# A two-layer diffusion backbone on one core: which modulation pairs, output products and attention steps run ahead of the gathers, and in what order

## Chip, core and metric

The kernel runs on 1 core of a Trainium2 chip. The metric is device time in microseconds (us) of one execution; the number given for a kernel is the median of several executions. All arithmetic is float32.

## The reference, cut to what matters

Two layers over 256 latent tokens and 256 context tokens of width 1024. Layer 0 has a gated-conv and spatial-gating mixer, layer 1 a conv module beside differential attention (4 heads); each is followed by PEER, a lookup of 128 expert rows per token. Every sub-layer is modulated by six vectors made from `c` (or `c_ctx`).

```python
for l in range(2):
    ada_x = (silu(c) @ w_ada[l] + b_ada[l]).reshape(1, 1, 6, 1024)
    ada_c = (silu(c_ctx) @ w_ada[l] + b_ada[l]).reshape(1, 1, 6, 1024)
    hx = modulate(rms_norm(x, norm1_g[l]), ada_x[:, :, 0], ada_x[:, :, 1])
    ...
    x = x + ada_x[:, :, 2] * yx
    h2 = modulate(rms_norm(x, norm2_g[l]), ada_x[:, :, 3], ada_x[:, :, 4])
    x = x + ada_x[:, :, 5] * peer(h2, ...)

def diff_attend(q, k, v, lam):           # layer 1, per head
    p = softmax(einsum(q, k) * 64 ** -0.5)
    return einsum(p[:, :, 0] - lam * p[:, :, 1], v)

def peer(h, wq, subkeys, u_tab, v_tab):  # per token
    q = h @ wq                           # 8 heads, 2 halves of 128
    s = q . subkeys; top 16 of each half; top 16 of their 256 sums -> idx, g
    return sum over the 128 idx of  g * gelu(h . u_tab[idx]) * v_tab[idx]
```

## The kernel before

**Stages and slots.** There are three stages of PEER work: stage 0 (latent tokens, layer 0), stage 1 (context tokens, layer 0), stage 2 (latent tokens, layer 1). Each has two tiles of 128 tokens, and each tile 128 slots. In a slot GpSimd issues one indirect DMA that gathers, for 128 tokens, one row of u and one of v (1 MB) into one of 8 ring slots of `uv`. VectorE multiplies u with the token row and sums (L1557, a dot), ScalarE makes a weight of it and a diagonal matrix (L1189 to L1193), and TensorE adds diag times v into two PSUM banks (`add_values`, L948), two slots later in its own program. 768 slots in all.

**Order.** `schedule()` writes one list, the program; every engine walks the same list and does its part of each step. A step may be "taken" (its PSUM bank emptied) later than it is issued. Dense steps are either placed between slots (`placed`, spread over a range of slots) or written out by hand in `before[stage]`, ahead of a stage's first slot. `before[0]` is the opening: nothing can be gathered until the first tile has passed through the mixer, the norm, `query`, `score` and the six parts of `find`, the search that writes `idx`. `before[2]` is the gap: the first tile of stage 2 needs the end of stage 1, the attention of layer 1 and the same chain. `deal(a, b)` spreads the steps b evenly among the steps a.

**Modulation vectors.** There are 12 pairs of columns per layer (a pair is two blocks of 1 MB, 8 KB per partition). A pair comes either on TensorE (`ada`, L680, then `ada_turn`, L695 and L696) or on VectorE (`ada_row`, L1250: a transposed block, two chunks, each multiplied with the two rows `c_rows` and summed). Layer 0 uses pairs 0 to 3 for shift and scale of the mixer, 4 and 5 for its gate, 6 to 9 for shift and scale of PEER, 10 and 11 for PEER's gate. `ADA_ROWS` says which pairs VectorE makes. `c_rows` is loaded by a DMA (L969) and passed through Silu on ScalarE (L1167) in step `mods`, just ahead of the first `norm`.

**Weights.** All blocks stream through the SyncE queue in program order (L983). `weight_places` gives each a place: 3 slots of `wring`, or, in the opening and in the gap, ring slots of `uv`. A block whose place is still held waits in the queue, and all behind it. In the gap the ring slots 2 to 5 may be used (`GAP_SLOTS`); slots 6 and 7 (`LATE_SLOTS`) hold the attention's `vc_rows[1]`, `orow[1]`, `pT`, `prob`, and their first gathers wait for step `o_turn` of the second tile, by this line of the GpSimd program:

```python
if T and s == LATE_SLOTS[0]:
    pool.wait_ge(*taken["orow", 1])
```

**Attention steps.** For i = 0 to 7 (tile, head): `scores` (PE, L836), `smax` (DVE, L1435), `soft` (ACT, L1095), `mix` (DVE, L1442 to L1444), `p_turn` (PE, L845), `value` (PE, L855). After a tile's four heads come `o_norm` (DVE), `o_turn` (PE, L871), and `out_half` (PE, L893; two halves b, four products each).

Of the kernel before, what the change touches and what calls it, by code (L numbers as in the profile page):

```python
# [43 lines left out]
ADA_ROWS = ((0, 10, 12), (1, 0, 6))  # L44
# [10 lines left out]

GAP_SLOTS = (2, 3, 4, 5)
LATE_SLOTS = (6, 7)
# [114 lines left out]
def kept_heads(stage):  # L172
# [6 lines left out]
         "rms_sum": 1.5, "rms_root": 1, "rms_scale": 1.5, "norm": 3, "out_half": 4, "turn_back": 2, "lam": 1, "conv": 2,  # L179
# [28 lines left out]
def schedule():  # L208
# [29 lines left out]

    early = [(0, 1, [mix[7], p_turn[7], value[7]]), (1, 2, [("o_norm", 2, 1)]), (2, 3, [("o_turn", 2, 1)]), (2, 10, find(2, 1, one)),
# [70 lines left out]
def weight_blocks(program):  # L310
# [3 lines left out]
    for i, (kind, item, *_) in enumerate(program):  # L314
# [7 lines left out]
        elif name == "out_half":  # L322
# [18 lines left out]
def weight_places(program, blocks):  # L341


    own, opening, gap = list(range(WRING)), list(range(WRING + RING)), list(range(WRING)) + [WRING + i for i in GAP_SLOTS]

    found = [program.index(("step", step)) for step in (("query", 0, 1, 0, (0,)), ("find", 2, 0, (0,), FIND_PARTS - 1))]
# [3 lines left out]
    for k, (_, _, _, first, last) in enumerate(blocks):  # L350
# [1302 lines left out]
```

## Time and profile before

| | |
|---|---|
| time, median of 3 runs | 2381.09 us (2379.73 to 2384.25) |
| the profiled execution: its own time, its span | 2382.0 us, 2380.2 us |
| PE, DVE, ACT, POOL busy | 2080.4 (87%), 1629.1 (68%), 961.4 (40%), 1021.0 (43%) us |
| DMA moved, mean | 940.46 MB, 395 GB/s |
| indirect gathers | 768, 805.36 MB |
| chain that ended last | PE 36%, DMA 29%, DVE 16%, issue 7%, POOL 6%, ACT 4% |

Times within the trace are counted from the start of its span. The span and 1.8 us around it make the execution's time. Busy time is the sum of an engine's instructions; the DMA share is the mean busy share of the core's 16 DMA engines.

### The profile page before, as it was taken

What the parts mean: (1) busy time and instruction counts of PE and PEld (TensorE: products, weight loads), DVE (VectorE), ACT (ScalarE), POOL (GpSimd) and SP (SyncE); (2) the same over time, 40 slices, a digit from 0 to 9 for tenths busy, and PEclk for the clock granted to TensorE, in tenths of its full rate; (3) what the DMA queues carried; (4) which work ended last, traced back from release to release, by engine and by line L of the source; (5) the groups of instructions that cost most, each with busy time, mean ns of one, the idle gap of its engine ahead of it and who ended that gap; (6) DMA issues with size and microseconds to landing.
All of it is one profiled execution on the core that took longest, in us unless ns stands there. A gap on an engine that the chain in (4) does not pass through costs nothing.

```text
span 2380.2 us, 23945 instructions
## 1 busy us (share of the span) xinstructions
PE 2080.4 (87%) x6792; PEld 1119.3 (47%) x6792; DVE 1629.1 (68%) x3980; ACT 961.4 (40%) x2788; POOL 1021.0 (43%) x868
## 2 busy tenths in 40 slices
PE   8988998899998988988899998898799987777777
PEld 6775554455564434544454454335456532222222
DVE  2876768967766568788856668754665887766444
ACT  2113434543334444444454334534443444443333
POOL 0002444444334544444445445520233555566774
PEclk9998999999999999999999999999899999999999
DMA  9968999999999999999999999994599999999997
GB/s 402 420 252 320 394 415 421 414 422 422 421 421 421 412 421 405 421 419 420 389 406 422 421 421 421 421 381 192 224 403 379 415 421 421 422 421 421 421 421 319
DMA packets 132738, 940.46 MB, mean 395 GB/s; under 512 B 14736, under 2 KB 17936, under 8 KB 18960
## 3 DMA queue, kind: packets, MB, share of 16 engines
q0 software_dynamic: 110592, 805.36, 82.0%
q1 hardware_dynamic: 22032, 133.73, 13.7%
q8 instruction: 54, 0.88, 0.1%
q14 instruction: 60, 0.49, 0.1%
HBM read 937.98 MB, written 1.05 MB: 395 GB/s over the span
## 4 chain that ended last, share of the span: by engine, by line
PE 36%; DMA 29%; DVE 16%; issue 7%; POOL 6%; ACT 4%; SPq 0%; POOLq 0%; DVEq 0%; ACTq 0%
DMA uv<-uv_dram,stage_idx 28%; PE psum L948 18%; PE psum L762 9%; POOL uv L1019 6%; DVE uv L1557 6%; PE psum L744 4%; DVE h L1250 2%; PE psum L893 1%; DMA h<-c_rows_dram 1%; ACT diag L1193 1%; ACT wv L1191 1%; PE psum L680 1%; ACT gel L1189 1%; DVE work L1521 0%; PE psum L922 0%
## 5 line engine op out<-in xcount | busy, mean ns | idle before, releaser
L948 PE MATMUL psum<-uv,diag 128*128 128x512 f32 x3072 | 1449.8, 612 | 240.0 <-ACT diag L1193 221.8
L1019 POOL DMA_INDIRECT uv<-uv_dram,stage_idx x768 | 987.2, 1285 | 1051.7 <-PE psum L948 823.7
L1557 DVE CUSTOM_DVE_ANT_0 uv<-uv,h 128x1024 f32<-128x1024 f32 x768 | 935.2, 1226 | 538.1 <-DMA uv<-uv_dram,stage_idx 527.4
L948 PEld LDWEIGHTS psum<-uv,diag 128*128 128x128 f32 x3072 | 562.7, 193 | 1023.7 <-issue 518.1
L1189 ACT ACTIVATE gel<-dots 128x1 f32<-128x1 f32 x768 | 156.3, 203 | 1052.4 <-DVE dots L1557 1050.2
L1193 ACT ACTIVATE diag<-const,wv 128x128 f32<-128x128 f32 x768 | 309.8, 403 | 24.8
L762 PE MATMUL psum<-hT,wring 128*128 128x256 f32 (+1 forms) x1280 | 266.2, 362 | 1.5 <-ACT hT L1060 1.5
L762 PEld LDWEIGHTS psum<-hT,wring 128*128 128x128 f32 x1280 | 227.9, 191 | 59.7 <-issue 33.0
L1191 ACT ACTIVATE wv<-gel,gw 128x1 f32<-128x1 f32 x768 | 228.0, 297 | 25.1
L1005 POOL COPY stage_idx<-idx 128x8 uint32 (+1 forms) x96 | 33.6, 350 | 284.6 <-DVE idx L1529 283.9
L1042 ACT ACTIVATE work<-psum 128x256 f32<-128x256 f32 (+2 forms) x122 | 47.8, 393 | 137.6 <-PE psum L762 108.5
L744 PE MATMUL psum<-wring,hT 128*128 128x256 f32 x320 | 75.1, 390 | 5.1 <-ACT hT L1060 5.1
L744 PEld LDWEIGHTS psum<-wring,hT 128*128 128x128 f32 x320 | 62.7, 196 | 21.6 <-issue 8.1
L1189 ACT ACT_TABLE_LOAD x51 | 65.4, 1283 | 0.9
L1557 DVE DVE_READ_ACCUMULATOR2_ANT dots<- 128x1 f32 x768 | 63.4, 83 | 0.0
L1250 DVE CUSTOM_DVE_ANT_0 h<-uv,h 128x1024 f32<-128x1024 f32 x44 | 52.2, 1223 | 9.7 <-DMA uv<-ada_t_dram 8.7
L762 PE MATMUL psum<-hT,uv 128*128 128x256 f32 (+1 forms) x256 | 54.8, 370 | 1.2 <-DVE sp_t L1332 1.2
L1497 DVE MAX8 work<-work 128x8 f32<-128x128 f32 x80 | 17.9, 282 | 52.8 <-ACT work L1042 52.8
L1369 DVE SCALAR_TENSOR_TENSOR work<-work,const 128x256 f32<-128x256 f32 x120 | 50.1, 480 | 0.0
L762 PEld LDWEIGHTS psum<-hT,uv 128*128 128x128 f32 x256 | 45.4, 190 | 8.5 <-issue 3.2
L1161 ACT ACT_TABLE_LOAD x32 | 41.1, 1283 | 0.6
L680 PE MATMUL psum<-uv,silu_c 128*32 128x256 f32 x400 | 30.4, 416 | 7.6 <-DMA uv<-ada_dram 7.6
(216 smaller groups left out, 1289.2 us busy)
## 6 DMA issues: line engine op xcount, KB each, us to landing
uv<-ada_dram SPq DMA_DIRECT2D x25, 1024.0 KB, 17.1
wring<-in_dram SPq DMA_DIRECT2D x24, 1024.0 KB
wring<-wq_dram SPq DMA_DIRECT2D x24, 1024.0 KB
uv<-uv_dram,stage_idx POOLq DMA_INDIRECT x768
uv<-ada_t_dram SPq DMA_DIRECT2D x11, 1024.0 KB, 16.7
uv<-in_dram SPq DMA_DIRECT2D x10, 1024.0 KB, 18.9
wring<-ada_dram SPq DMA_DIRECT2D x7, 1024.0 KB
wring<-ada_t_dram SPq DMA_DIRECT2D x5, 1024.0 KB
```

What stands on the lines that cost most here:

```text
L680: last = mm(bank[QW * q:QW * (q + 1), 0:BLK], silu_c[:, kq, :], kc(("ada", i))[:, kq, :], start=(k == 0), stop=(k == KC // 2 - 1))
L744: last = mm(bank[:, 0:BLK], src[:, k, :], w[:, k, :], start=(k == 0), stop=(k == KC - 1))
L762: last = mm(bank[:, 0:len(tiles) * P], w[:, k, i * P:(i + 1) * P], hT[:, k, tokens], start=(k == 0), stop=(k == KC - 1))
L948: last = mm(acc[:, b, :], diag[:, s % RING, :], uv[:, s % RING, D + 512 * b:D + 512 * (b + 1)], start=(c == 0), stop=(c == NSEL - 1))
L1019: nc.gpsimd.indirect_dma_start(out=uv[:, s, :], out_offset=None, in_=tables[stage // 2], in_offset=bass.IndirectOffsetOnAxis(ap=stage_idx[ ...
L1042: mine.emptied(f(dst, src, func, **kw))
L1189: f(gel[:, r:r + 1], dots[:, r:r + 1], ACT.Gelu_apprx_tanh).then_inc(gelu_ready, 1)
L1191: f(wv[:, r:r + 1], gel[:, r:r + 1], ACT.Copy, scale=gw[:, (T // TT) % 2, T % TT, c:c + 1]).then_inc(wv_ready, 1)
L1193: f(diag[:, r, :], C("ident"), ACT.Copy, scale=wv[:, r:r + 1]).then_inc(diag_ready, 1)
L1250: v.tensor_tensor_reduce(out=row_tmp[:, j, :], in0=w, in1=c_rows[:, j, :], scale=1.0, scalar=0.0, op0=ALU.mult, op1=ALU.add, accum_out=ada ...
L1369: ops = [v.scalar_tensor_tensor(out=ccT[:, j, :], in0=cpT[:, j, k:k + TOK], scalar=w[:, j, k:k + 1], in1=ccT[:, j, :], op0=ALU.mult, op1=A ...
L1557: v.tensor_tensor_reduce(out=uv[:, r, 0:D], in0=uv[:, r, 0:D], in1=h2[:, row_of[stage], t, :], scale=1.0, scalar=0.0, op0=ALU.mult, op1=AL ...
```

## The change

**Opening.** VectorE now makes layer 0's pairs 4 to 9, and no pair of layer 1; TensorE makes layer 0's pairs 10, 11 and layer 1's 0 to 7. In all there are 12 VectorE blocks in place of 16, and 28 TensorE blocks ahead of the first slot in place of 24. Ahead of the first tile's output products stand only five TensorE pairs (eight before); pair 3 of layer 1 is dealt among these products, 4 and 5 stand around the norm, 6 and 7 behind the second head's score. The second tile's output products (`out_rows(0, 1)`) move into slots 0 to 2, `turn_back` behind the first head's score, and the heads of the second tile start at slot 8 instead of 3. The four `out_w` blocks take ring slots 4 to 7. `c_rows` is made by 16 small products and four PSUM copies (`vector_rows`) in place of the DMA and the Silu; the opening idle products are 10 in place of 28.

**Gap.** `LATE_SLOTS` and its wait are gone: `vc_rows[1]` and `orow[1]` move to `gate_peer`, `pT` to `wst`, `prob` to the context rows of `x`, and ring slots 2 to 7 all take weight blocks. The norm's root comes ahead of pair 8, pair 9 moves behind the output products, 10 idle products stand ahead of pair 8. The first tile's `o_norm`, `o_turn` and output products go in two halves, heads 0 and 1, then 2 and 3 (`out_heads`: both column blocks are open at once in two PSUM banks). `scores`, `smax`, `soft` of the second tile move behind; of that tile's attention, `mix` 6 to `value` 7 now lie in slots 0 to 4, with its `o_norm` in slots 5 to 7 and `o_turn` in 7 to 8.

```diff
-ADA_ROWS = ((0, 10, 12), (1, 0, 6))
+ADA_ROWS = ((0, 4, 10),)
+LAST_SLOTS = (4, 5, 6, 7)
-GAP_SLOTS = (2, 3, 4, 5)
-LATE_SLOTS = (6, 7)
+GAP_SLOTS = (2, 3, 4, 5, 6, 7)
...
-        0: [("idle", 28)] + ada(0, 0, 2) + rms(0) + [("idle", 14)] + ada(0, 2, 3)[:1] + [("idle", 6)] + ada(0, 2, 4)[1:] + [("mods", 0, 0)]
-        + norm(0, 0)
-        + deal(deal(project_even(0) + gate(0, 0) + out_rows(0, 0), [s for layer, first, last in ADA_ROWS for s in ada_rows_of(layer, first, last)]),
-               ada(0, 4, 10) + ada(1, 6, 8)) + [("mods", 0, 1)]
-        + rms(0, one) + out_rows(0, 1)[:1] + norm(0, 1)[:1] + [("turn_back", 0, 0)] + query(0, 0, one) + score(0, 0, one)
-        + find(0, 0, one) + out_rows(0, 1)[1:] + query(0, 1, one) + score(0, 1, one) + find(0, 1, one)[:2],
+        0: [("c_rows", 0, 0), ("c_rows", 0, 1), ("c_rows", 1, 0), ("c_rows", 1, 1), ("idle", 10)] + ada(0, 0, 2) + rms(0)
+        + [("idle", 14)] + ada(0, 2, 3)[:1] + [("idle", 6)] + ada(0, 2, 4)[1:] + [("mods", 0, 0)] + norm(0, 0)
+        + deal(deal(mixing[:-4] + [gates[0], mixing[-4], gates[1], gates[2], mixing[-3], gates[3]] + mixing[-2:],
+                    [step for layer, first, last in ADA_ROWS for step in ada_rows_of(layer, first, last)]),
+               ada(0, 10, 12) + ada(1, 0, 3))
+        + deal(out_rows(0, 0), ada(1, 3, 4)) + [("mods", 0, 1)] + rms(0, one) + ada(1, 4, 6)[:2] + norm(0, 1)[:1] + ada(1, 4, 6)[2:]
+        + query(0, 0, one) + score(0, 0, one) + [("turn_back", 0, 0)] + find(0, 0, one)[:4] + query(0, 1, one) + score(0, 1, one)
+        + ada(1, 6, 8) + find(0, 0, one)[4:] + find(0, 1, one)[:3],
...
-        2: [root, ("ada", 1, 8)] + rms(1, (1,)) + [("kc_turn", 2, 0), ("norm_ctx", 2, 1), ("ada", 1, 9)]
+        2: [root] + rms(1, (1,)) + [("idle", 10), ("ada", 1, 8), ("kc_turn", 2, 0), ("norm_ctx", 2, 1)]
...
-        + [p_turn[2], scores[4], mix[3], value[2], p_turn[3], value[3], smax[4], root, ("o_norm", 2, 0)]
-        + [("ada_turn", 1, 8), ("ada_turn", 1, 9), ("o_turn", 2, 0), exp, soft[4], mix[4], out_t[0][0], ("mods", 2, 1), out_t[0][1]]
-        + [p_turn[4], scores[5], root] + rms(2, one) + [value[4], exp] + norm(2, 1)[:1] + [smax[5]] + query(2, 0, one)[:1] + [soft[5]]
...
+        + [p_turn[2], root, mix[3], value[2], p_turn[3], ("o_norm", 2, 0, 0, 2), value[3], ("o_turn", 2, 0, 0, 2)]
+        + [("out_heads", 2, 1, b, 0, 0, 2) for b in range(2)] + [("o_norm", 2, 0, 2, 4), ("o_turn", 2, 0, 2, 4)]
+        + [("out_heads", 2, 1, b, 0, 2, 4) for b in range(2)] + [("ada", 1, 9)] + rms(2, one)
+        + [("ada_turn", 1, 9), scores[4], ("mods", 2, 1)] + norm(2, 1)[:1] + [exp, smax[4], soft[4], ("idle", 4)]
+        + query(2, 0, one) + [mix[4]] + score(2, 0, one) + [p_turn[4], value[4], ("turn_back", 2, 0)] + search[:4]
+        + [scores[5], ("ada", 1, 10)] + query(2, 1, one) + score(2, 1, one) + [("ada_turn", 1, 10), ("ada", 1, 11), scores[6], ("ada_turn", 1, 11)]
+        + search[4:] + [smax[5], soft[5], smax[6], soft[6], mix[5], p_turn[5]],
...
-    early = [(0, 1, [mix[7], p_turn[7], value[7]]), (1, 2, [("o_norm", 2, 1)]), (2, 3, [("o_turn", 2, 1)]), (2, 10, find(2, 1, one)),
+    early = [(0, 4, [mix[6], p_turn[6], scores[7], value[5], smax[7], soft[7], value[6], mix[7], p_turn[7], value[7]]),
+             (5, 7, [("o_norm", 2, 1, 0, HEADS)]), (7, 8, [("o_turn", 2, 1, 0, HEADS)]), (3, 10, find(2, 1, one)),
...
-            own = early if stage else [(0, 3, find(0, 1, one)[2:])]
-            for first, last, steps in own + heads_by_tile(stage, own[-1][1]) + kept_heads(stage):
+            own = early if stage else [(0, 2, find(0, 1, one)[3:]), (0, 2, out_rows(0, 1))]
+            for first, last, steps in own + heads_by_tile(stage, 12 if stage else 8) + kept_heads(stage):
...
-        vc_rows = [view(work, 5956, MIX), slot(6, 0, MIX)]
+        vc_rows = [view(work, 5956, MIX), gate_peer[:, 0:MIX]]
-        orow = [slot(1, 0, MIX), slot(6, MIX, MIX)]
-        pT = slot(6, 1024, 2, MIX)
-        prob = slot(7, 0, 2, 2, MIX)
+        orow = [slot(1, 0, MIX), gate_peer[:, MIX:]]
+        pT = wst.rearrange("p (a b) -> p a b", a=2)
+        prob = x[:, 0:TT, :].rearrange("p a (b c) -> p a b c", b=2)
...
+            def vector_rows(vector, half):
...
+                bank = to_act.open(pe)
+                for i in range(4):
+                    last = mm(bank[:, i * P:(i + 1) * P], silu_c[:, 4 * half + i, vector:vector + 1].to_broadcast([P, P]), ident,
+                              start=True, stop=True)
...
-                            if T and s == LATE_SLOTS[0]:
-                                pool.wait_ge(*taken["orow", 1])
```

## Rows read from the trace of the kernel before

**Rows 1.** The profile's page, part 2: DMA share in tenths and GB/s, 40 slices.

```profile
DMA  9968999999999999999999999994599999999997
GB/s 402 420 252 320 394 415 421 414 422 422 421 421 421 412 421 405 421 419 420 389 406 422 421 421 421 421 381 192 224 403 379 415 421 421 422 421 421 421 421 319
```

**Rows 2.** Windows: busy time by engine, then PEclk, DMA share, GB/s, two stretches.

```profile
190.00:1590.00 1400.00, 1265.24 (x3743) 678.93 (x3742) 1008.37 (x2486) 607.59 (x1771) 642.61 (x574) 0.98 1.01 415
1590.00:1710.00 120.00, 93.30 (x537) 63.81 (x536) 59.76 (x142) 49.05 (x119) 7.02 (x9) 0.84 0.51 202
```

**Rows 3.** Windows, same columns: short stretches of the opening and of the gap.

```profile
38.00:46.00 8.00, 7.86 (x23) 6.40 (x24) 4.17 (x8) 3.16 (x7) 0.00 (x0) 0.62 1.02 418
150.00:160.00 10.00, 10.00 (x52) 8.90 (x51) 8.15 (x15) 0.18 (x1) 0.00 (x0) 1.00 0.49 195
160.00:170.00 10.00, 7.09 (x40) 5.91 (x38) 8.87 (x22) 2.92 (x7) 0.00 (x0) 1.00 0.00 0
1650.00:1660.00 10.00, 9.83 (x35) 4.93 (x33) 5.34 (x10) 3.34 (x7) 0.00 (x0) 0.91 0.00 0
```

**Rows 4.** Timeline from 31 us: start, duration, engine, line, operands, idle before.

```profile
31.14 1.95 PE L728 MATMUL psum<-const,work 128*128 128x128 f32 x16
...
34.78 1.91 ACT L1167 ACTIVATE h<-h 128x2048 f32<-128x2048 f32 x1 [1.99 <-DMA h<-c_rows_dram]
...
38.15 13.56 PE L744 MATMUL psum<-wring,hT 128*128 128x256 f32 x48 [5.06 <-ACT hT L1060]
```

**Rows 5.** Timeline, 133 to 190 us, PE, DVE, POOL, to the first gather.

```profile
133.78 1.93 PE L680 MATMUL psum<-wring,silu_c 128*32 128x256 f32 x32
...
138.12 1.16 PE L714 MATMUL psum<-gdiag,ones 128*128 128x128 f32 x8 [2.41 <-DVE gdiag L1268]
...
146.68 7.17 PE L744 MATMUL psum<-uv,work 128*128 128x256 f32 x32
...
165.30 1.23 DVE L1276 CUSTOM_DVE_ANT_0 work<-x 128x1024 f32<-128x1024 f32 x1
...
170.67 1.94 PE L903 MATMUL psum<-const,hT 128*128 128x128 f32 x8 [1.58 <-ACT hT L1060]
...
187.04 0.17 DVE L1529 SCALAR_TENSOR_TENSOR idx<-work 128x16 uint32<-128x16 f32 x1
...
188.55 1.16 POOL L1019 DMA_INDIRECT uv<-uv_dram,stage_idx  x1 [0.97 <-PE psum L744]
```

**Rows 6.** Line 1250 alone: duration of one, min, median and max in ns.

```profile
L1250 DVE CUSTOM_DVE_ANT_0 h<-uv,h x44: 1218/1224/1229, 51.0 to 163.8; 128x1024 f32<-128x1024 f32 x44
```

**Rows 7.** Timeline after the first gather: first product of values, ninth gather.

```profile
199.14 6.37 PE L948 MATMUL psum<-uv,diag 128*128 128x512 f32 x8 [6.07 <-issue]
...
203.72 1.05 POOL L1019 DMA_INDIRECT uv<-uv_dram,stage_idx  x1 [4.63 <-PE psum L948]
```

**Rows 8.** Timeline of the gap, 1600 to 1710 us.

```profile
1601.75 3.64 PE L680 MATMUL psum<-wring,silu_c 128*32 128x256 f32 x32 [3.25 <-DMA wring<-ada_dram]
...
1611.67 10.63 PE L744 MATMUL psum<-uv 128*128 128x256 f32 x48
...
1648.45 8.78 PE L893 MATMUL psum<-wring,work 128*128 128x512 f32 x16 [0.69 <-ACT work L1042]
...
1658.79 1.23 DVE L1276 CUSTOM_DVE_ANT_0 work<-x 128x1024 f32<-128x1024 f32 x1
...
1679.49 0.96 POOL L1019 DMA_INDIRECT uv<-uv_dram,stage_idx  x1 [0.83 <-POOL stage_idx L1005]
...
1689.43 0.17 DVE L1442 RECIPROCAL prec<-psums 128x2 f32<-128x2 f32 x1 [9.01 <-ACT uv L1095]
...
1708.52 0.94 POOL L1019 DMA_INDIRECT uv<-uv_dram,stage_idx  x1 [18.67 <-PE psum L871]
```

**Rows 9.** Windows, same columns: soon after each restart of the gathers.

```profile
220.00:240.00 20.00, 19.63 (x84) 13.36 (x83) 5.43 (x13) 5.38 (x19) 4.74 (x6) 1.00 0.89 324
1830.00:1850.00 20.00, 20.00 (x70) 11.76 (x69) 10.21 (x31) 7.25 (x24) 8.25 (x9) 1.00 0.89 330
```

More of the change, by code:

```diff
@@ L349, in weight_places @@
     until, holds, places, previous = [-1] * (WRING + RING), [None] * (WRING + RING), [], []
-    for k, (_, _, _, first, last) in enumerate(blocks):
+    for k, (kind, _, _, first, last) in enumerate(blocks):
         if first < first_slot:
-            allowed = opening if last < found[0] else own
+            allowed = opening if last < first_slot else own
+            if kind == "out_w":
+                allowed = [WRING + i for i in LAST_SLOTS]
         elif gap_close < first < gap_slot:
-            allowed = gap if last < found[1] else own
+            allowed = gap if last < found else own
         else:
@@ L398, in build @@
         ss_heads, ms_heads, root_heads = (sb(s, [P, 16]) for s in ("ss_heads", "ms_heads", "root_heads"))
-        smax, nmax, psums, prec = (sb(s, [P, 2, 2]) for s in ("smax", "nmax", "psums", "prec"))
+        smax, nmax, psums = (sb(s, [P, 2, 2]) for s in ("smax", "nmax", "psums"))
+        prec = sb("prec", [P, TT * HEADS, 2])
         uv = sb("uv", [P, RING, 2 * D])
@@ L865, in conv_root, with o_turn @@
                 to_dve.fill(last)
-            def o_turn(stage, t):
-                pe.wait_ge(on_ready, t + 1)
+            def o_turn(stage, t, first, last):
+                pe.wait_ge(on_ready, n.up("on_ready"))
                 bank = to_act.open(pe)
-                for h in range(HEADS):
-                    last = turn(bank[:, h * P:(h + 1) * P], orow[t][:, h * P:(h + 1) * P], ident)
-                to_act.fill(last)
-                taken["orow", t] = (act_bank_full, to_act.n)
+                for h in range(first, last):
+                    done = turn(bank[:, (h - first) * P:(h - first + 1) * P], orow[t][:, h * P:(h + 1) * P], ident)
+                to_act.fill(done)
+                n["oT", t, last] = to_act.n
             def out_rows(stage, b, t):
@@ L928, in score @@
                     taken["scores", k, t] = (act_took, to_act.n)
-            steps = {"idle": idle, "ada": ada_pair, "ada_turn": ada_turn, "ada_row": ada_row, "gate": gate, "norm": turn_rows, "norm_ctx": turn_rows,
+            steps = {"idle": idle, "c_rows": vector_rows, "ada": ada_pair, "ada_turn": ada_turn, "ada_row": ada_row, "gate": gate, "norm": turn_rows, "norm_ctx": turn_rows,
                      "v_rows": v_project, "u_cols": noted("u_cols"), "ah_cols": noted("ah_cols"), "cg_cols": noted("cg_cols"),
@@ L1131, in conv_out_step, with o_turn @@
                 act.wait_ge(conv_out, 1)
-            def o_turn(stage, t):
-                empty(yT[:, MC:, t * P:(t + 1) * P], 4 * P, a=HEADS)
+            def o_turn(stage, t, first, last):
+                empty(yT[:, MC + first:MC + last, t * P:(t + 1) * P], (last - first) * P, a=last - first)
             def turn_back(stage, t):
@@ L1177, in _ @@
                      "value": value, "conv_sum": conv_sum, "conv_root": lambda stage: root(rr_root[:, :], rr_ms[:, :]),
-                     "conv_out": conv_out_step, "o_norm": lambda stage, t: root(rr_o[:, :], ms_o[:, :]), "o_turn": o_turn,
+                     "conv_out": conv_out_step,
+                     "o_norm": lambda stage, t, first, last: root(rr_o[:, first:last], ms_o[:, first:last]), "o_turn": o_turn,
                      "turn_back": turn_back, "find": find}
@@ L1548, in _ @@
             takes = {"ac_cols": ac_cols, "spatial": spatial, "ab_cols": ab_cols, "ca_cols": ca_cols, "out_rows": out_rows,
-                     "out_half": out_half}
+                     "out_half": out_half,
+                     "out_heads": lambda stage, half, b, t, first, last: last == MC and out_half(stage, half, b, t)}
             def dot(s):
```

108 lines of the change are left out of this document (59 added, 49 removed).

## Prediction

> **What bounds the kernel now.** I read the page first. Its DMA line shows some 421 GB/s in most slices, with three holes: slices 3 and 4, slices 27 to 29, and the last [rows 1]. 940.46 MB at 421 GB/s are 2234 us, so 146 of the 2380 us are missing DMA time, and a 1.05 MB gather or block is 2.49 us of DMA. Next I read windows over the stages: from 190 to 1590 us the DMA share is 1.01, from 1590 to 1710 it is 0.51 [rows 2]. Ten-us windows split the first hole: the weight loads end near 155 us, then nothing moves [rows 3] until the first gather is issued at 188.55 [rows 5]. So the time is the bytes plus the stretches in which the DMA has no work, and a change counts only by how it moves the first gather of stage 0 and of stage 2, or by holes it makes later. The second thing to see is that TensorE is busy 1265 of 1400 us in the full stretch [rows 2]: little room is left there for work moved behind a first gather. The chain of waits and the timelines of PE, ACT, DVE and POOL then gave the steps ahead of both first gathers [rows 4, 5, 8].
>
> **The opening, up to the first gather.** All blocks needed there are the same 56 before and after, so an earlier first gather is gained in full, as long as the loads are done by then.
> - `c_rows`. The first rows were turned at 33.1 us, but ScalarE waited for the load of `c_rows` and made its Silu until 36.7, and the first product followed at 38.15 [rows 4]. Modulating one tile takes 38.15 - 36.7 = 1.5 us, and the first tile's turns are done at half of the 1.95 us, at 32.1: the products can start at 33.6 to 33.8. Gain 4.4. The 16 new products and the idle ones are 26 in place of 28, and lie ahead of a pair that waits for its blocks anyway; I put them at nothing.
> - Clock. From 38 to 46 us the granted clock was 0.62 after 5.06 us of idle PE [rows 3, 4]; 48 products took 13.56 us, at the rate of 7.17 for 32 [rows 5] they take 10.8. Gain 2.8, since the idle time goes. [...]
> - Pairs. Five TensorE pairs in place of eight ahead of the output products, 1.93 us each [rows 5]: gain 5.8.
> - VectorE rows. Four blocks less, 4 instructions of 1.22 us each [rows 6]: 19.6 us less on DVE, which had made PE wait 2.4 us for the first gate half [rows 5]. Gain 2.4.
> - The pairs' small turns, the wait before the second gate half and the lowered clock behind it have no price above. I take 5 for them, bounds 0 and 6.
> - Sum 20.4: the output products start at 126.3 in place of 146.7.
> - From there to the norm's first instruction it was 18.6 us [rows 5]; four products at 7.17 / 2, one pair and the adding make 17.2. Gain 1.4. `turn_back` (1.94 us [rows 5]) leaves the chain. Pairs 4 and 5 (3.9 us) stand ahead of the norm's turns, the norm's own DVE work covers some 2.9 of them: loss 1.
> - The first gather then comes 20.4 + 1.4 + 1.9 - 1.0 = 22.7 us earlier, at 165.9.
> - Cover: the loads ended at 155, and without `c_rows` at 152.5. The blocks of pairs 4 and 5 are followed by six more, so they land by 152.5 - 6 x 2.49 = 137.6, and PE wants them at 143. Without that cover each late block costs 2.5.
>
> **Behind the first gather.** Four products of the second tile (14.3 us of PE) come behind it. Before, PE idled 6.07 us ahead of its first values product, 10.6 us after the first gather; the ninth gather went at +15.2 [rows 5, 7]. Now PE makes pairs 6 and 7, then the products; the fourth needs a bank that DVE empties only behind the second dot, so the values start near +16 and the ninth gather goes near +18. Eight gathers and one block are 22.4 us of DMA, so this is covered. On the SyncE queue the third head's block waits for the place of pair 7, made just before the products, so it lands among the first gathers; the keys behind it wait as before. The ring slot of the fourth `out_w` block is free at +16, when six gathers and the block (17.4 us) run out at +18.4: covered by 2 us. But the second tile's heads now start at slot 8 with the same work, and soon after the restart the share is 0.89 in 20 us already [rows 9], a loss of 2.2. I take 2 more; bounds 0 and 14.3 (nothing hidden). Opening: 20.7.
>
> **The gap.** From 1590 to 1710 the DMA idled 0.49 x 120 = 58.8 us [rows 2].
> - Pair 8 ran at 3.64 us after 3.25 us of idle PE; warm it is 1.93 [rows 5, 8]: 1.7. Pair 9 leaves the way: 1.9 to 2.8. The norm's root no longer waits behind pair 8's copy. The context products move from 1611.7 to 1606.6: 5.1.
> - The output products took 8.78 us and the norm began at 1658.79 [rows 8]. Now half of them run while heads 2 and 3 are normalized, and `scores` and `smax` 4 are behind. On the old clock of the gap: first halves 1644.0 to 1647.4, second `o_turn` copied at 1648.2, second halves at warm rate to 1651.6, adding to 1653.1. Gain 5.6.
> - The first gather of stage 2 moves from 1679.5 to 1668.8.
> - Loads: nine places in place of seven are free at the start, the attention frees the rest, so all 16 blocks and two key loads (40.8 us of DMA) are done before, three of them came behind it. From 1594 to the first gather's start (1669.8) that leaves 35.0 us idle, with 3.4 before 1594 it is 38.4.
> - The gathers of slots 6 and 7 waited 18.67 us for the second tile's `o_turn` [rows 8], which nothing does now; that hole is part of the 58.8.
> - Gain 20.4. Against it: that tile's last attention steps, `o_norm` and the search of the second head now share slots 0 to 10 with the dots, some 31 us of DVE in 30 us, and each is a round trip of three engines. Late next are the ninth gather and those that follow. I take 4, bounds 0 and 14. Gap: 16.4.
>
> Total 37.1: 2382.0 - 37.1 = 2344.9 for the profiled execution; the median lies 0.9 below that execution's time, so 2344.
>
> **Rivals.**
> - *PE has no room behind the first gather.* For it: PE busy 90% [rows 2] and 0.89 of DMA in the 20 us after the restart [rows 9]. Against: DMA is full from there to 1590 nevertheless. The 14.3 us of products come back: 2356.
> - *The leftover attention sets the pace of the gap.* For it: `mix` 5 waited 9.0 us for `soft` [rows 8], and DVE is full in those slots. Against: in the gap's hole no dots were in the way of such waits, and none of these steps was needed for a gather. Only the earlier first gather (10.7) less 4 stays of 16.4: about 2354. Both together: 2365.
> - *More is gained.* Neither give-back (6 us) happens and the small turns count in full: 2336.
> - *Slower.* Each of the five DVE steps among slots 0 to 8 (`mix` 6, `smax` 7, `mix` 7, two parts of `o_norm`) holds the dots behind it for a full round trip. It decides from 37.1 / 5 = 7.4 us each beyond what the ring covers; the longest seen is 9.0. At 9.0: 45 us back, 2389.
> - *The order does nothing*, because blocks land later than PE wants them: needs some nine blocks late. The queue is full until 155 and blocks are placed as before; small.
>
> **How the numbers follow.** Chances: forecast (2338 to 2350) 0.45; PE without room 0.17; attention sets the pace 0.17; both 0.06; more gained 0.10; slower 0.03; nothing 0.02. The time is that of the likeliest, 2344. The range takes in both single give-backs and the better case: 2334 to 2359. A measurement tells about 0.2% (4.8 us) from no change; the cases sum to faster 0.95, same 0.02, slower 0.03.
>
> **What would show it.** First `ada_row` and first product near 34 us with the clock at 1.00; output products from about 126; first indirect DMA near 166, ninth within 20 us of it, DMA share at 0.9 or more from there. In the gap: context products near 1606 less the opening's gain, first gather some 75 us after the last of stage 1 landed (85 before), no wait of POOL over 7 us among its first 16 gathers. Wrong it is if the opening's first product does not move, if DVE, not PE, sets the mixer's pace, or if windows of 20 us behind either restart show a DMA share under 0.8.

## The result, and the profile of the changed kernel

The changed kernel takes 2365.84 us (median of 4 runs, 2362.31 to 2366.76) against 2381.32 us: a ratio of 0.9931, interval 0.9914 to 0.9948. It is 16 us faster, in the direction forecast, but far less than the forecast 37 and outside the range (2334 to 2359). The profiled execution took 2366.4 us, span 2364.6, so 15.6 us less than the one of before.

The page of the changed kernel, DMA share and GB/s in 40 slices [rows 1]:

```profile
DMA  9979999999999999999999999996699999999997
GB/s 402 375 304 373 388 395 421 402 421 421 421 420 421 408 421 405 421 421 413 401 388 420 421 422 421 421 383 261 275 366 383 415 421 422 421 421 421 422 420 317
```

The first hole is now shared out over slices 2 to 6: 304 where 252 was, but 375 where 420 was and 388 where 394 was. That is the first thing to see: the DMA's missing time was moved more than removed. Windows of the same kernel, busy time by engine, then PEclk, DMA share, GB/s [rows 2, 3]:

```profile
34.00:42.00 8.00, 8.00 (x38) 7.05 (x37) 5.79 (x12) 2.76 (x6) 0.00 (x0) 1.00 1.02 417
100.00:110.00 10.00, 7.20 (x35) 5.77 (x34) 9.48 (x23) 0.18 (x1) 0.00 (x0) 0.97 1.01 422
110.00:120.00 10.00, 8.65 (x61) 6.50 (x60) 9.79 (x22) 0.98 (x2) 0.00 (x0) 0.86 0.39 147
...
170.00:180.00 10.00, 10.00 (x103) 7.92 (x96) 7.09 (x30) 2.58 (x6) 4.10 (x5) 1.00 0.55 178
190.00:200.00 10.00, 10.00 (x26) 6.38 (x25) 7.96 (x19) 3.60 (x12) 2.52 (x4) 0.76 0.54 197
1590.00:1710.00 120.00, 98.19 (x585) 67.78 (x586) 73.34 (x192) 56.53 (x138) 17.41 (x19) 0.93 0.66 263
```

The timeline of the opening (PE, SyncE, DVE, POOL), start and duration in us [rows 4, 5]:

```profile
33.73 14.05 PE L768 MATMUL psum<-wring,hT 128*128 128x256 f32 x64 [0.71 <-ACT hT L1091]
51.16 7.14 PE L786 MATMUL psum<-hT,uv 128*128 128x256 f32 x32 [1.51 <-DMA uv<-in_dram]
...
99.67 0.43 SPq L1016 DMA_DIRECT2D uv<-ada_t_dram  x1
116.53 0.81 SPq L1016 DMA_DIRECT2D uv<-out_w_dram  x2
...
109.23 5.38 PE L786 MATMUL psum<-hT,uv 128*128 128x256 f32 x16 [2.80 <-DVE sp_t L1364]
117.82 1.16 PE L738 MATMUL psum<-gdiag,ones 128*128 128x128 f32 x8 [1.34 <-DVE gdiag L1300]
124.33 1.16 PE L738 MATMUL psum<-gdiag,ones 128*128 128x128 f32 x8 [1.90 <-DVE gdiag L1300]
135.62 7.15 PE L768 MATMUL psum<-uv,work 128*128 128x256 f32 x32
152.97 1.22 DVE L1308 CUSTOM_DVE_ANT_0 work<-x 128x1024 f32<-128x1024 f32 x1
174.24 1.09 POOL L1050 DMA_INDIRECT uv<-uv_dram,stage_idx  x1 [0.97 <-PE psum L704]
```

The first product comes at 33.73 at full clock (1.00 from 34 to 42), as forecast. Then TensorE waits three times for VectorE, 6.0 us in all, and VectorE is busy 9.5 and 9.8 of 10 us from 100 to 120; the output products start at 135.62 (forecast 126.3). The SyncE queue stands for 17 us, because the next block's place is not free. The first gather goes at 174.24 (forecast 165.9, before 188.55).

The same kernel behind the first gather (DVE, PE, POOL) [rows 7]:

```profile
187.26 1.23 DVE L1593 CUSTOM_DVE_ANT_0 uv<-uv,h 128x1024 f32<-128x1024 f32 x1
...
188.41 0.42 DVE L1499 TENSOR_TENSOR work<-psum,gate_mix 128x256 f32<-128x256 f32 x1
...
188.89 6.61 PE L768 MATMUL psum<-uv,work 128*128 128x256 f32 x16 [3.20 <-DVE work L1499]
195.34 1.88 PE L983 MATMUL psum<-uv,diag 128*128 128x512 f32 x4
...
196.34 0.97 POOL L1050 DMA_INDIRECT uv<-uv_dram,stage_idx  x1 [10.70 <-PE psum L768]
...
199.78 0.96 POOL L1050 DMA_INDIRECT uv<-uv_dram,stage_idx  x1 [0.83 <-POOL stage_idx L1038]
```

The fourth output product of the second tile waits until VectorE has emptied the first one's bank. That stands behind the end of the second head's search and the second dot, at 188.41. The wait is 3.20 us and the product then runs at a lowered clock (0.52 from 190 to 195; 6.61 for 3.6 us). The seventh gather needs the fourth block's ring slot and goes at +22.1 (forecast +16), the ninth at +25.5 (forecast near +18).

The gap of the changed kernel (PE, DVE, POOL) [rows 8]:

```profile
1603.29 3.69 PE L768 MATMUL psum<-wring,uv 128*128 128x256 f32 x16 [1.51 <-ACT uv L1091]
...
1630.79 0.71 PE L881 MATMUL psum<-vx,wst 128*128 128x128 f32 x4 [2.52 <-ACT wst L1073]
...
1647.18 1.22 DVE L1308 CUSTOM_DVE_ANT_0 work<-x 128x1024 f32<-128x1024 f32 x1
...
1668.11 0.96 POOL L1050 DMA_INDIRECT uv<-uv_dram,stage_idx  x1 [0.83 <-POOL stage_idx L1038]
...
1685.88 0.96 POOL L1050 DMA_INDIRECT uv<-uv_dram,stage_idx  x1 [7.43 <-PE psum L983]
...
1697.07 1.16 POOL L1050 DMA_INDIRECT uv<-uv_dram,stage_idx  x1 [7.63 <-PE psum L983]
```

The wait of 18.67 us is gone, two of 7.4 and 7.6 us stand in its place. Below, the last dot of stage 1 (1594.23 before, 1590.49 after) divides the execution; d76 is the dot of slot 76 (416.41 before, 410.22 after).

| | before | after | gain | forecast |
|---|---|---|---|---|
| first gather | 188.55 | 174.24 | 14.3 | 22.7 |
| first gather to d76 | 227.9 | 236.0 | -8.1 | -2 |
| d76 to last dot of stage 1 | 1177.8 | 1180.3 | -2.5 | 0 |
| last dot of stage 1 to first gather of stage 2 | 85.3 | 77.6 | 7.6 | 10.7 |
| from there to the last dot | 690.8 | 686.6 | 4.2 | 5.7 |

### The profile page after: what moved, and what is told of

It is laid out like the page before. It is cut to its first block, busy times and chain, and to the rows that moved or that the text cites. A ratio compares the mean times of both kernels' runs of the same rounds, so it can differ in the third digit from the quotient of the medians.

```text
span 2364.6 us, 24131 instructions
## 1 busy us (share of the span) xinstructions
PE 2085.6 (88%) x6896; PEld 1127.7 (48%) x6896; DVE 1610.6 (68%) x3952; ACT 957.0 (40%) x2794; POOL 1007.9 (43%) x868
## 4 chain that ended last, share of the span: by engine, by line
PE 29%; DMA 25%; DVE 10%; issue 6%; POOL 6%; ACT 4%; POOLq 0%; SPq 0%; DVEq 0%; ACTq 0%
DMA uv<-uv_dram,stage_idx 25%; PE psum L983 17%; PE psum L786 6%; POOL uv L1050 6%; DVE uv L1593 5%; PE psum L768 3%; PE psum L926 1%; ACT diag L1225 1%; ACT wv L1223 1%; ACT gel L1221 0%; ACT L1221 0%; DVE work L1556 0%; PE psum L862 0%; PE psum L957 0%; PE psum L704 0%
## 5 line engine op out<-in xcount | busy, mean ns | idle before, releaser
L786 PE MATMUL psum<-hT,wring 128*128 128x256 f32 (+1 forms) x1312 | 273.0, 362 | 0.7 <-ACT hT L1091 0.7
L786 PEld LDWEIGHTS psum<-hT,wring 128*128 128x128 f32 x1312 | 233.6, 191 | 59.4 <-issue 33.4
L1282 DVE CUSTOM_DVE_ANT_0 h<-uv,h 128x1024 f32<-128x1024 f32 x28 | 33.2, 1223 | 2.8 <-issue 2.1
L957 PEld LDWEIGHTS psum<-keys,work 128*128 128x128 f32 x192 | 26.1, 194 | 18.1 <-issue 11.5
```

Of the source, the lines that this page charges most:

```text
L786: last = mm(bank[:, 0:len(tiles) * P], w[:, k, i * P:(i + 1) * P], hT[:, k, tokens], start=(k == 0), stop=(k == KC - 1))
L1282: v.tensor_tensor_reduce(out=row_tmp[:, j, :], in0=w, in1=c_rows[:, j, :], scale=1.0, scalar=0.0, op0=ALU.mult, op1=ALU.add, accum_out=ada ...
```

## The experiments

All ratios are to the kernel before, with the 95% interval; differences between two kernels come from their ratios times 2381 us. Rows of single executions scatter: the same stretch from d76 to the end of stage 1, with the same steps in it, took 1177.8 to 1183.7 us over all the kernels here, and the medians decide where a profiled execution says otherwise. The stretch from the first gather to d76 took 232.1, 232.8 and 233.5 us in three more executions with the changed opening (pe_load_late_twice, opening_alone, pe_load_late, below), so the 8.1 us of the table is the highest of four: what was given back there is 4 to 8 us.

**Which half carries it.** opening_alone has all the diff's edits of the opening, gap_alone all of the gap.

> The kernel before with the whole opening of the changed one (rows and pairs, c_rows on TensorE, order, out_w places, second tile's products in slots 0 to 2) and the old gap. Theory A, read from the two traces: the first gather comes 14.3 us earlier, but some 10.6 of it is given back behind it, because TensorE has no room there; the last values of stage 1 came 3.7 us earlier in the changed kernel, so this one takes 2376 to 2378 us (3 to 5 less than before), with the first gather near 174.2 and the last values of stage 1 near 1592.8. Rival B, the opening keeps most of its 14.3 and the gap loses: 2367 to 2369. Rival C, the opening is worth nothing by itself: 2380 to 2383.

Measured: 2375.44 us, 0.9971 (0.9960 to 0.9983), 7 us less; first gather at 174.30, seventh at +22.5.

> The kernel before with the whole gap of the changed one (six ring places, buffers moved, output products by pairs of heads, leftover attention in slots 0 to 8) and the old opening. Theory A: the gap carries most of the change, 11 to 13 us: 2368 to 2370 us; from the last values of stage 1 to the first gather of stage 2 some 75 us in place of 83, and no wait of GpSimd of 18 us for the second tile's turn. Rival B, the gap is worth nothing or loses and the opening carries it: 2380 or more. Rival C, the forecast's size: 16 us or more, 2365 or less.

Measured: 2371.24 us, 0.9948 (0.9934 to 0.9962), 12.4 us less. From the last dot of stage 1 to the last dot of all it took 764.2 us, as in the changed kernel (764.3), against 776.1 before and 776.7 in opening_alone. So the gap is worth 12 and the opening 4 to 7 (7 by itself, 4 on top of the gap, which the intervals don't tell apart).

**The fourth product's wait.**

```diff
-        + ada(1, 6, 8) + find(0, 0, one)[4:] + find(0, 1, one)[:3],
+        + ada(1, 6, 8) + find(0, 0, one)[4:] + find(0, 1, one)[:3] + out_rows(0, 1)[:2],
...
-            own = early if stage else [(0, 2, find(0, 1, one)[3:]), (0, 2, out_rows(0, 1))]
+            own = early if stage else [(0, 2, find(0, 1, one)[3:]), (0, 2, out_rows(0, 1)[2:])]
```

> The changed kernel with one edit: the first two output products of the second tile, and so VectorE's adding of them, stand at the end of the opening, ahead of slot 0's dot and of the last parts of the second head's search; the other two stay in slots 0 to 2. The order on TensorE stays, but the fourth product no longer waits 3.2 us for VectorE and runs warm (3.6 for 6.6 us). Theory A, TensorE is what the slots behind the first gather go by: the gather of slot 6 moves from +22.1 to about +16 behind the first gather, the first values from +21.1 to +15, and 5 to 6 us of it stay to the end: 2359 to 2361 us. Rival B, the DMA queue or the later slots set the pace whatever happens here: within 1.5 us of the changed kernel, 2364.5 to 2366. Rival C, VectorE waits for products ahead of the search and the dots, and it is slower by 2 or more.

Measured: 2362.60 us, 0.9911 (0.9896 to 0.9926), 4.8 us less than the changed kernel, though the two intervals overlap. Its timeline (POOL, PE):

```profile
176.09 1.10 POOL L1050 DMA_INDIRECT uv<-uv_dram,stage_idx  x1 [0.97 <-PE psum L704]
...
176.93 14.06 PE L768 MATMUL psum<-uv,work 128*128 128x256 f32 x64
190.83 3.60 PE L983 MATMUL psum<-uv,diag 128*128 128x512 f32 x8
...
191.83 0.94 POOL L1050 DMA_INDIRECT uv<-uv_dram,stage_idx  x1 [4.68 <-PE psum L768]
```

The four products run in one piece and the seventh gather goes at +15.7. From the first gather to d76 (405.40) it takes 229.3 us, 1.4 more than before the change and not 4 to 8, with the same four products behind the first gather. The fourth product waited 1.9 to 4.0 us for VectorE in all six profiled executions with the changed kernel's order, and not at all here: most of the give-back was this one wait.

**VectorE ahead of the output products.** In rows_spread, `ada_rows_of(0, 4, 9)` is dealt among the mixer and the four chunks of pair 9 among `out_rows(0, 0)`.

> The changed kernel with one edit: of the 24 VectorE chunks of pairs 4 to 9, the four of pair 9 (9.8 us of VectorE) are dealt among the first tile's output products and no longer among the mixer's. Theory A, VectorE was behind ahead of the output products (its 9.48 and 9.79 us of 10 from 100 to 120, TensorE's waits of 2.80, 1.34 and 1.90 us and the lowered clock after them): the waits vanish, the output products start at 127 to 129 in place of 135.6, the SyncE hole from 99.7 to 116.5 shrinks, the first gather comes at 166 to 169, and 4 to 8 us stay at the end (2358 to 2362 us). Rival B: the output products start earlier, but the gain is all given back behind the first gather, for TensorE has no room there: 2364.5 to 2366. Rival C, TensorE or the loads are what the mixer waits for: the output products start after 134.

Measured: 2364.78 us, 0.9924 (0.9910 to 0.9937), 1.7 us less than the changed kernel, which the intervals don't tell from nothing. The output products do come at 129.84 (127.8 to 130.5 in all ten profiled executions with these rows moved, 135.6 to 137.5 in the seven with the changed kernel's), but the first gather only at 173.86. Its timeline and one window:

```profile
129.84 7.15 PE L768 MATMUL psum<-uv,work 128*128 128x256 f32 x32
...
152.43 1.41 PE L752 MATMUL psum<-const,work 128*128 128x128 f32 x8 [2.09 <-DVE work L1317]
```

```profile
150.00:160.00 10.00, 7.91 (x47) 7.57 (x40) 3.40 (x9) 2.60 (x9) 0.00 (x0) 0.66 0.97 380
```

At the norm's turns TensorE now waits 2.09 us, and the granted clock is 0.66 from 150 to 160, just where the query's products lie. Also, its fourth `out_w` block fell into ring slot 4, so its fifth gather waited 14.90 us. Both were tried next.

```diff
-                    [step for layer, first, last in ADA_ROWS for step in ada_rows_of(layer, first, last)]),
+                    ada_rows_of(0, 4, 9)),
...
-        + deal(out_rows(0, 0), ada(1, 3, 4)) + [("mods", 0, 1)] + rms(0, one) + ada(1, 4, 6)[:2] + norm(0, 1)[:1] + ada(1, 4, 6)[2:]
+        + deal(out_rows(0, 0), ada_rows_of(0, 9, 10)[:2] + ada(1, 3, 4)[:1] + ada_rows_of(0, 9, 10)[2:] + ada(1, 3, 4)[1:])
+        + [("mods", 0, 1)] + rms(0, one) + ada(1, 4, 6)[:2] + [("idle", 10)] + norm(0, 1)[:1] + ada(1, 4, 6)[2:]
```

This and the two takes are opening_mended; mended_without_idle leaves out the `idle` step.

> The changed kernel with three edits: the first two output products of the second tile ahead of slot 0 (as in two_takes_ahead), pair 9's VectorE chunks dealt among the first tile's output products (as in rows_spread), and 10 idle products between pairs 4 and 5 and the norm's turns, so that the clock does not fall there as it did in rows_spread. Theory A, TensorE's waits and its slow stretches are what is lost ahead of slot 53: output products near 130, first gather at 168 to 171, 6 to 9 us under the changed kernel: 2357 to 2360 us. Rival B, only the take order counts: 2361 to 2362, as two_takes_ahead. Rival C, the fourth out_w block now lies in ring slot 4 and holds the gathers from the fifth on: 2364 or more.

> opening_mended without its 10 idle products between pairs 4 and 5 and the norm's turns. Theory A, in rows_spread TensorE waited 2.09 us there and the granted clock was 0.66 from 150 to 160, which ate the 5.8 us that the output products had come earlier; the same comes back: clock 0.6 to 0.7 in that stretch, first gather 2 to 4 us later than in opening_mended (171.35), and 2 to 4 us more at the end (2358 to 2360). Rival B, the idle products do nothing, and it was the two takes and the rows together: 2355.5 to 2357.

Measured: opening_mended 2356.26 us, 0.9889 (0.9875 to 0.9903), 10 us less than the changed kernel; without the idle products 2360.25, 0.9908 (0.9893 to 0.9923), 4.5 more, though these two intervals overlap. The window of opening_mended, then that of mended_without_idle:

```profile
150.00:160.00 10.00, 9.63 (x97) 8.86 (x89) 3.95 (x11) 3.06 (x11) 0.00 (x0) 1.00 0.97 383
```

```profile
150.00:160.00 10.00, 9.31 (x54) 9.32 (x55) 2.00 (x5) 2.22 (x8) 0.00 (x0) 0.66 1.01 412
```

From the output products to the first gather the first takes 40.9 us (130.45 to 171.35), the second 44.0 (128.10 to 172.12): ten idle products of 0.24 us each in a wait that is there anyway are worth 3.1 us. That is no scatter: the stretch took 40.9 us in all six executions with them and the `out_w` places of opening_mended, and 44.0 in both without (rows_spread is the other).

**c_rows by itself** (the 16 products and the copies, 10 idle products for 28, on the kernel before).

> The kernel before with one edit: c_rows comes from the 16 small products and four PSUM copies (28 idle products become 10), not from the load and its Silu. Theory A, TensorE sets the pace from the first product on: the first product comes at 33.7 in place of 38.15 at full clock, its chain gains 4.4 to 7.2 us less what VectorE makes it wait, and 3 to 6 us stay to the end (2376 to 2379 us). Rival B: the first product comes early, but VectorE's rows (behind in the mixer already) take it back: the output products start within 1 us of 146.7 and the time is 2381 to 2383.

Measured: 2379.19 us, 0.9988 (0.9980 to 0.9997), 2.9 us less. Its timeline:

```profile
33.86 10.60 PE L754 MATMUL psum<-wring,hT 128*128 128x256 f32 x48 [0.71 <-ACT hT L1068]
46.08 1.93 PE L690 MATMUL psum<-uv,silu_c 128*32 128x256 f32 x32 [1.62 <-DMA uv<-ada_dram]
...
53.82 1.93 PE L690 MATMUL psum<-uv,silu_c 128*32 128x256 f32 x32 [2.16 <-DMA uv<-ada_dram]
...
144.21 6.09 PE L754 MATMUL psum<-uv,work 128*128 128x256 f32 x27
```

The 7.2 us forecast (4.4 and the clock's 2.8) are all there at the first product and its rate. Waits for blocks take 3.8 of them at once, and the output products come 2.5 us earlier (146.68 to 144.21). Neither theory as written: what is left is about what VectorE gained at its start (its first row instruction at 35.20 for 37.41).

**Has TensorE room behind the first gather?** Idle products, six groups over slots 14 to 40 or over 64 to 100: 30 (7.3 us) and 60 (14.6 us), added to the changed kernel.

```diff
+    placed += spread([("idle", 10)] * 6, 14, 40)
```

> The changed kernel with 30 more idle products of 128 columns on TensorE (0.24 us each, 7.3 us), six groups of five spread over slots 14 to 40. Theory A, from the first product to about slot 53 TensorE's own work sets the pace (busy 294.4 of 316.3 us from 33.7 to 350 in the changed kernel, 291.0 of 317.9 in the one before): 5 to 7 us slower than the changed kernel, 2371 to 2373. Rival B, the DMA queue sets the pace there and TensorE has room: within 1.5 us.

> The changed kernel with the same 30 idle products, spread over slots 64 to 100. Theory A: there the DMA queue sets the pace and TensorE has room, so no more than 1.5 us slower than the changed kernel (2365 to 2367.5). Rival B, TensorE sets the pace throughout stage 0: 5 to 7 us slower, as with the products in slots 14 to 40.

> The changed kernel with 60 more idle products (14.6 us of TensorE), six groups of ten over slots 14 to 40. With 30 of them there it took 4 us more, and 5 us more than with 30 in slots 64 to 100. Theory A, TensorE sets the pace up to about slot 53: 10 to 14 us over the changed kernel, ratio to the kernel before 0.997 to 1.000. Rival B, the 4 us were scatter and TensorE has room: within 3 us of the changed kernel.

> The changed kernel with the same 60 idle products over slots 64 to 100. Theory A, the DMA queue sets the pace there and most of it is hidden: 0 to 4 us over the changed kernel, ratio 0.993 to 0.995. Rival B, TensorE sets the pace throughout stage 0: 10 to 14 us over it, as in slots 14 to 40.

Measured: early 2367.14 (0.9948, 0.9935 to 0.9962) and 2370.38 (0.9954, 0.9941 to 0.9967), 4.0 and 5.5 us over the changed kernel; late 2363.95 (0.9926, 0.9913 to 0.9939) and 2364.03 (0.9924, 0.9910 to 0.9937), none. Windows of the changed kernel, of pe_load_early_twice, of pe_load_late_twice:

```profile
218.00:305.00 87.00, 81.61 (x319) 52.31 (x318) 51.02 (x138) 36.24 (x110) 33.36 (x30) 1.00 0.99 396
```

```profile
218.00:305.00 87.00, 85.56 (x385) 58.36 (x384) 49.52 (x134) 33.41 (x101) 29.91 (x28) 1.00 0.95 374
```

```profile
218.00:305.00 87.00, 81.61 (x315) 51.89 (x314) 52.15 (x140) 36.70 (x113) 33.38 (x30) 1.00 1.00 403
```

Late, 14.6 us cost nothing. Early, 14.6 us cost 5.5; the intervals of the early ones overlap with the changed kernel's, but the two kernels with 60 products are apart (0.9941 and up against 0.9937 and down): TensorE had some room (5.4 us idle in this stretch) and no more, and with it gone the DMA share falls to 0.95. Theory A's 10 to 14 us was too much.

**The places of the out_w blocks** (5, 6, 4, 7 by column block in place of 7, 6, 5, 4, on opening_mended).

```diff
-                allowed = [WRING + i for i in LAST_SLOTS]
+                allowed = [WRING + LAST_SLOTS[column]]
```

> opening_mended with the four out_w blocks put into ring slots 5, 6, 4 and 7 by column block (there they fell to 7, 6, 5 and 4, so that the fourth block held ring slot 4 and the fifth gather waited 10.9 us for its product). Theory A: the fifth gather goes at +11 or +12 in place of +15.7 behind the first one, the hole in the DMA behind the fourth gather shrinks by 3 to 4 us, and 1 to 3 us stay to the end (2353.5 to 2355.5). Rival B: the blocks land later, because ring slot 4 is free later, and TensorE waits for them at the output products: no change or slower (2356 to 2359). Rival C: TensorE's order sets the pace there, and earlier gathers only wait longer for their values: 2355.5 to 2357.

Measured: 2365.19 us, 0.9929 (0.9916 to 0.9943), 9.5 us more than opening_mended: rival B. SyncE queue, PE, and one window:

```profile
98.28 0.33 SPq L1016 DMA_DIRECT2D uv<-ada_t_dram  x1
123.42 0.33 SPq L1016 DMA_DIRECT2D uv<-out_w_dram  x1
...
157.20 3.27 PE L704 MATMUL psum<-uv,silu_c 128*32 128x256 f32 x32 [3.04 <-DMA uv<-ada_dram]
```

```profile
110.00:120.00 10.00, 7.02 (x23) 6.08 (x24) 9.02 (x22) 0.88 (x2) 0.00 (x0) 0.66 0.00 0
```

The fifth gather does go at +12.3. But the queue waits 25 us for the first block's place, all behind it land late, and the first gather comes at 180.85.

**The rest,** each on opening_mended: the gap's root table behind value 2 (root_later); the second tile's attention over slots 0 to 10 (leftover_spread); its heads of stage 0 from slot 3 (mended_heads_at_3); the last two together (best_a), and with 12 more idle products ahead of the first gate half (best_b); all_mended is mended_places with leftover_spread.

> opening_mended with one edit in the gap: the loading of the root's table stands behind value 2 and no longer ahead of it. Theory A: the load of 1.28 us made TensorE wait 2.52 us for ScalarE's copy of the turned probabilities just ahead of the first tile's o_turn, and it lies on the chain to the norm: the first gather of stage 2 comes 76 us after the last dot of stage 1 in place of 77.6 to 77.9, 1 to 2 us less in all (2354 to 2355.5 us). Rival B: the root's load is then late for o_norm, which waits as long: no change, 2356 to 2357.

> opening_mended with one edit behind the gap: mix 6 to value 7 of the second tile spread over slots 0 to 7 in place of 0 to 4, its o_norm in slots 7 to 9 and o_turn in 9 to 10. Theory A: these steps are round trips of three engines, they hold the dots (GpSimd waits of 7.1 and 8.2 us for values at the ninth and eleventh gather), and farther apart they hold them less: from the first gather of stage 2 to slot 528's dot 57 us or less in place of 59.4, and 1 to 3 us less in all (2353 to 2355 us). Rival B: the same steps with the same round trips only come later: 59 to 60 us, no change or a little slower (2356 to 2359).

> opening_mended with the second tile's heads of stage 0 starting at slot 3, as in the kernel before, not at slot 8. Theory A: with the four products also in slots 0 to 2 too much of TensorE and VectorE stands among the first dots, so slot 45's dot comes no earlier and the time is the same or 1 to 3 us more (2356 to 2359). Rival B: spread over 36 slots and not 31, the heads leave more room: 1 to 3 us less (2353.5 to 2355.5).

> mended_places and leftover_spread together: the opening mended, the out_w blocks placed by column block, and mix 6 to o_turn of the second tile spread over slots 0 to 10 behind the gap. leftover_spread alone moved slot 528's dot from 59.4 to 58.2 us behind the first gather of stage 2 and did not change the median. Theory A: the sum of both, 2352.5 to 2355.5 us. Rival B: neither is worth anything that can be measured: 2355.5 to 2357.5.

> opening_mended with the second tile's heads of stage 0 from slot 3 (as in mended_heads_at_3) and the second tile's attention spread over slots 0 to 10 behind the gap (as in leftover_spread). Neither changed the median by itself, though both moved later dots forward in their profiled executions (slot 76 from 403.3 to 397.6; the end from 762.6 to 762.3 behind stage 1). Theory A, they are worth 1 to 3 us together: 2353 to 2355 us, ratio 0.988. Rival B, neither is worth anything: 2355.5 to 2357.5, ratio 0.989.

> best_a with 12 more idle products on TensorE ahead of the first gate half, where it waited 3.15 us for VectorE and the granted clock was 0.66 from 110 to 120. Theory A, the lowered clock there costs about 1 us on the gate half (2.08 for 1.16 us) and 1.8 on the products behind it (5.54 for 3.70), and comes back: the output products start at 128 in place of 130.5, and 1 to 3 us less than best_a. Rival B, VectorE's rows are what the mixer waits for, so TensorE only waits longer at the next place: within 1.5 us of best_a. Rival C, the idle products hold up the gate half: slower.

| | us | ratio | interval |
|---|---|---|---|
| root_later | 2357.72 | 0.9900 | 0.9883 to 0.9916 |
| leftover_spread | 2356.36 | 0.9887 | 0.9872 to 0.9903 |
| mended_heads_at_3 | 2354.93 | 0.9891 | 0.9876 to 0.9906 |
| all_mended | 2362.62 | 0.9921 | 0.9908 to 0.9935 |
| best_a | 2353.55 | 0.9882 | 0.9866 to 0.9899 |
| best_b | 2353.52 | 0.9879 | 0.9863 to 0.9896 |

None is told from opening_mended but all_mended, which carries the bad places. root_later kept the wait of 2.52 us that it was to remove and made the next one 1.60 us (0.69 in opening_mended), so the table load (1.28 us) is not its cause. best_b's output products came at 127.83 and best_a's at 129.02, and nothing of it is seen at the end. best_a, 28 us under the kernel before and 12 under the changed one, and opening_mended are the versions that beat both.

## Why the prediction was wrong

By the prediction's own steps, in profiled executions (forecast 37.1, measured 15.6; the rows of the table above miss 21.5):

- **The step that failed first, 8.4 us of the first gather:** the sum 20.4 that brings the output products to 126.3. 11.1 came, 9.3 less, and 0.9 of that came back behind them. Its parts for `c_rows`, clock, pairs and rows were added up as gains of TensorE's own chain. Windows from the first product to the output products, before, then after:

```profile
38.15:146.68 108.53, 102.26 (x657) 81.42 (x657) 86.38 (x181) 14.87 (x35) 0.00 (x0) 0.94 1.01 420
```

```profile
33.73:135.62 101.89, 93.36 (x552) 76.61 (x553) 76.67 (x164) 13.45 (x30) 0.00 (x0) 0.97 0.95 394
```

 The first product gained 4.4. TensorE's busy time, the small turns in it, fell by 8.9, where clock and pairs alone had been taken at 8.6. What failed are the two terms for its waits, "Gain 2.4" for the first gate half and the "5" for the small turns, the second gate half's wait and the lowered clock (0.67 from 140 to 150 before): TensorE idled 8.5 us in place of 6.3. Its waits for VectorE are 6.0 us and were 5.5 (2.41 and these two), and it waits 2.5 us for blocks in place of 0.7:

```profile
118.01 3.69 PE L762 MATMUL psum<-hT,uv 128*128 128x256 f32 x16 [1.22 <-DVE sp_t L1332]
...
141.20 2.07 PE L714 MATMUL psum<-gdiag,ones 128*128 128x128 f32 x8 [1.92 <-DVE gdiag L1268]
```

 So VectorE set the mixer's pace, which the prediction had named as what would make it wrong. How many of its row instructions stood ahead of the output products is in the line's own view, first before (up to 146.68), then after (up to 135.62):

```profile
L1250 DVE DVE_READ_ACCUMULATOR2_ANT ada_c<- x56: 79/83/93, 38.6 to 145.9; 128x1 f32 x56
```

```profile
L1282 DVE DVE_READ_ACCUMULATOR2_ANT ada_c<- x46: 79/83/89, 36.2 to 134.3; 128x1 f32 x46
```

 The prediction took 16 off; of those only 10 stood ahead of that point (56 to 46), 12.2 us. VectorE also started 2.3 us earlier, but it waited 3 us more itself (108.53 - 86.38 = 22.2 us idle before, 101.89 - 76.67 = 25.2 after). What TensorE saved it could use only as far as VectorE came forward. rows_spread takes 8 more away and 5.8 us come; c_rows_alone leaves 2.5 of its 7.2.
- **c_rows and the clock:** both sizes right (33.73 and 1.00), but "ahead of a pair that waits for its blocks anyway" was applied to the small products only, and holds for the gain too.
- **From the output products to the first gather:** norm after 17.35 us (forecast 17.2); from there 21.3 against 22.4. Right.
- **The second step that failed, 6.1 us in the changed kernel's profile, 2 to 6 by the four executions:** "the ring slot of the fourth `out_w` block is free at +16 ... covered by 2 us". The order was seen right (the bank is emptied behind the second dot), but that dot is itself behind the rest of the second head's search, which the sum had left out. With that wait away, in two_takes_ahead, 1.4 us are given back, within the 2 forecast.
- **PE has no room** (rival, 0.17): not as written. 14.3 us of products cost 1.4 (two_takes_ahead), and 14.6 more in slots 14 to 40 cost 5.5. It has little room, and only there.
- **Cover of the loads:** it held in the changed kernel: though the queue stood for 17 us, TensorE waited for none of the blocks behind that; mended_places shows how near the edge it was (25 us of standing cost 9.5).
- **The gap, 4.6 us too much:** 11.8 of 16.4. Context products gained 4.6 against stage 1's end (forecast 5.1), the norm 7.9 (10.7): TensorE's 2.52 us for ScalarE (1.45 at the same head before) and a clock of 0.66 from 1630 to 1640, where the first halves took 4.73 us for the 3.70 of the second ones. In the trace ScalarE makes a head's exponentials until 1630.14, just ahead of the copy that TensorE waits for; no run moved them, so that cause is not shown. No wait of GpSimd over 7 us was forecast; there are two, of 7.43 and 7.63.
- **d76 to the end of stage 1, 2.5 us:** this much and more is scatter; gap_alone, with the old opening, took 1181.1 there. Not settled further.

That both give-backs come true had been priced at 2365 (its own terms, 12.3 and 9.7 over 2344, make 2366). That this is the time measured is luck: the first gather was late, which that rival did not have.

## What to carry to other kernels

Before adding up what several removed steps save, ask which engine's instructions fill the stretch, and count how many of those (not of the whole change) stand ahead of the point of interest: gains on two engines in one stretch were no sum here (20.4 us forecast for the output products, 11.1 came). Where a product needs a bank that another engine must empty (a wait of 3.20 us in the changed kernel), list all that stands in front of the emptying in that engine's order, searches and dots too. And a wait that is removed in one place can leave TensorE waiting at the next, as the 2.09 us at the norm's turns in rows_spread: ten idle products inside that wait went with a granted clock of 1.00 from 150 to 160 (0.66 without them), and the stretch up to the first gather was 3.1 us shorter.

## What the hardware showed

- One wait of TensorE of 2.09 us for VectorE stands ahead of a stretch with a mean granted clock of 0.66 (rows_spread and mended_without_idle, 150 to 160). In rows_spread the clock is 1.00 from 140 to 152, 0.50 from 154 to 159 and 1.00 again from 160. With ten idle products of 0.24 us each inside the same wait the clock stayed at 1.00 (opening_mended, 150 to 160). That a wait stands ahead does not settle the clock behind it: the one of 3.15 us at the first gate half went with 0.66 from 110 to 120 in rows_spread and with 1.00 in mended_without_idle, and no run shows why.
- Where its timeline shows no wait, VectorE was busy 9.5 to 9.9 of 10 us (changed kernel, 100 to 120; kernel before, 120 to 140). From 100 to 110 in the changed kernel a share of 0.95 (9.48 us) went with no wait at all.
